# A two-layer hybrid decoder step: row-wise products that end tile by tile, a layer norm per row tile, earlier activations and regrouped transposes

## The reference

```python
def run_layer(l, x, buf_a, buf_b, h0, mem_k, mem_v):
    mix, nb_a, nb_b, h_last = token_mixing(x, ...)      # convolution, recurrence, cross-attention, w_mix_out
    x = layer_norm(ALPHA * x + mix, ln1_g[l], ln1_b[l])
    if l % 2 == 0:
        f = swiglu(x, w_ff_gate[j], w_ff_up[j], w_ff_down[j])      # d_ff = 2816
    else:
        f = moe_swiglu(x, w_router[j], ...)                        # 8 experts, top 2
    x = layer_norm(ALPHA * x + f, ln2_g[l], ln2_b[l])
```

## Time and profile before

| | us |
|---|---|
| median of 3 runs (2096.21 to 2097.61) | 2096.25 |
| profiled execution, its own time | 2094.53 |
| its span in the trace | 2092.8 |
| TensorE busy | 1944.9 (93%) |
| VectorE busy | 1488.1 (71%) |
| ScalarE busy | 1055.6 (50%) |
| GpSimd busy | 106.3 (5%) |

### The profile page before, as it was taken

The page is one execution under the profiler, slowest core; times in us unless marked ns, Lnnn a source line. Parts: engine busy times, 40 slices in busy tenths (PEclk is TensorE's granted clock), DMA queues, the critical chain, the costliest instruction groups (busy, mean ns, idle before and its releaser), DMA issues. The chain is left out here.

```text
span 2092.8 us, 27971 instructions
## 1 busy us (share of the span) xinstructions
PE 1944.9 (93%) x10429; PEld 1647.8 (79%) x10430; DVE 1488.1 (71%) x2049; ACT 1055.6 (50%) x1150; POOL 106.3 (5%) x157
## 2 busy tenths in 40 slices
PE   7999889899997999988969999999999999999990
PEld 7889789699986978978956677878787878776670
DVE  6977685565525988656567567888888888876664
ACT  4443644333322445373325445776777677665541
POOL 2000000000001020000000001010101010100000
PEclk9999999999999999999979999999999999999995
DMA  7543434254432553433337567898989898986413
GB/s 289 187 169 126 141 122 147 88 173 148 151 123 81 202 192 133 171 111 132 131 127 258 196 220 278 338 369 342 366 337 371 336 369 337 373 335 233 184 51 118
DMA packets 118597, 447.43 MB, mean 214 GB/s; under 512 B 10368, under 2 KB 10368, under 8 KB 117872
## 3 DMA queue, kind: packets, MB, share of 16 engines
q1 hardware_dynamic: 112128, 423.66, 55.7%
q0 software_dynamic: 6384, 22.64, 2.9%
HBM read 437.52 MB, written 11.36 MB: 214 GB/s over the span
## 5 line engine op out<-in xcount | busy, mean ns | idle before, releaser
L594 DVE TENSOR_TENSOR wpl<-e_ring,wph 128x2048 fp32r<-128x2048 f32 x269 | 605.8, 2286 | 87.0 <-ACT wph L588 85.4
L588 ACT CAST wph<-e_ring 128x2048 fp32r<-128x2048 f32 x269 | 502.1, 1904 | 119.8 <-PE psum L1867 66.9
L550 DVE TENSOR_TENSOR wl<-ring,wh 128x1024 fp32r<-128x1024 f32 x234 | 285.7, 1223 | 260.1 <-ACT wh L544 258.7
L1641 PE MATMUL psum<-xTh,wh 128*128 128x320 f32 x1184 | 379.2, 320 | 36.8 <-DVE xTl L1174 13.2
L1643 PE MATMUL psum<-xTh,wl 128*128 128x320 f32 x1184 | 371.3, 314 | 0.0
L1642 PE MATMUL psum<-xTl,wh 128*128 128x320 f32 x1184 | 371.2, 313 | 0.0
L544 ACT CAST wh<-ring 128x1024 fp32r<-128x1024 f32 x234 | 244.1, 1045 | 163.0 <-PE psum L1658 91.8
L1865 PE MATMUL psum<-wph,xe 128*128 128x512 f32 (+1 forms) x768 | 295.4, 385 | 3.7 <-issue 3.4
L1866 PE MATMUL psum<-wph,xe 128*128 128x512 f32 (+1 forms) x768 | 290.8, 379 | 0.0
L1867 PE MATMUL psum<-wpl,xe 128*128 128x512 f32 (+1 forms) x768 | 290.8, 379 | 0.0
L1641 PEld LDWEIGHTS psum<-xTh,wh 128*128 128x128 f32 x1184 | 227.6, 192 | 44.0 <-issue 18.4
(11 more groups left out here) (305 smaller groups left out, 2639.7 us busy)
## 6 DMA issues: line engine op xcount, KB each, us to landing
e_ring<-experts SPq DMA_DIRECT2D x264, 1024.0 KB, 6.1
ring<-stream SPq DMA_DIRECT2D x274, 512.0 KB, 3.3
lnp<-rows POOLq DMA_DIRECT2D x4, 1024.0 KB, 5.7
arena<-out_rows SPq DMA_DIRECT2D x6, 512.0 KB, 8.0
x<-x POOLq DMA_DIRECT2D x3, 512.0 KB, 13.4
arena<-x0T POOLq DMA_DIRECT2D x1, 1280.0 KB, 8.7
o_a<-arena POOLq DMA_DIRECT2D x2, 540.0 KB, 6.0
o_k<-arena POOLq DMA_DIRECT2D x2, 512.0 KB, 3.5
```

Of the source, the lines that this page charges most:

```text
L550: dve.tensor_tensor(wl[:, q % SPLITS, :], ring[:, u % SLOTS, :], wh[:, q % SPLITS, :].bitcast(F32), ALU.subtract).then_inc(lo_done, 1)
L588: act.copy(wph[:, SLOT_OF[m % NPOS], :], ring_place(m).rearrange("p u c -> p (u c)")).then_inc(hi_e, 1)
L594: dve.tensor_tensor(wpl[:, s, :], ring_place(m).rearrange("p u c -> p (u c)"), wph[:, s, :].bitcast(F32), ALU.subtract).then_inc(lo_e, 1)
L1641: pe.matmul(out, h[:, k], hi[:, k], start=(k == 0), stop=False)
```

## The change

Six edits, all in the order of work:

- `rows_of` and `Plan.rows`: the last `LAST` = 3 units are no longer used one after the other for all tiles. Unit by unit up to the fourth last; then for each row tile the three last units together. Tiles end three units' work apart instead of one's.
- `residual` does residual, statistics (`spread`) and scale (`scaled`) for one tile before the next; `normalise` is gone. At the last norm the statistics are all made first.
- the splits ahead of the norm are bounded by `last_rows`, the step at which the third last unit is used up, where the step of a tile's end stood.
- `layer_norm_std` runs a 1 x 1 square root ahead of its first wait for a variance, and with it the table load.
- the start: `x0T` is loaded by SP in two halves behind the first unit; one unit is split, four k of xTh/xTl made, the next unit split, the other four k made, the third unit split. x is loaded by GpSimd after keys and values are evacuated.
- `rows_turned` does all transposes of 128 rows of a group and then those of 32; `clear_down` multiplies zero tiles of 128 partitions.

```diff
@@ Plan.rows
-        for k in range(n_units - 1):
+        for k in range(n_units - LAST):
             self.step((), (l, name, k), split=True)
         for t in TURN:
-            last = t == TURN[-1]
-            self.step([(l, name, 2 * t), (l, name, 2 * t + 1)], (l, name, n_units - 1) if last else None, split=last)
+            if t == TURN[-1]:
+                for k in range(n_units - LAST, n_units - 1):
+                    self.step((), (l, name, k), split=True)
+            self.step([(l, name, 2 * t), (l, name, 2 * t + 1)],
+                      (l, name, n_units - 1) if t == TURN[-1] else None, split=t == TURN[-1])
@@ layer_norm_std
             act.wait_ge(eps_ready, 1)
+            act.activation(turn_top[0:1], ones[0:1, 0:1], ACT.Sqrt)
@@ sync
                 sp.dma_start(ring[:, u % SLOTS, :], stream[u]).then_inc(slot_full[u % SLOTS], 16)
+                if u == 0:
+                    for k in range(0, KT, 4):
+                        sp.dma_start(cb[:, k:k + 4], x0T[:, k:k + 4]).then_inc(xt_in[k // 4], 16)
@@ gpsimd
-            pool.dma_start(cb, x0T).then_inc(xt_in, 16)
...
                 for n in range(2):
                     emptied(pool, l, "v", n)
+                if l == 0:
+                    for t, r0 in enumerate(TOK):
+                        pool.dma_start(x[:, t, :], x0[r0:r0 + P]).then_inc(x_in, 16)
@@ scalar (vector alike, with make_lo and xTl)
-            for _ in range(SPLITS):
-                make_hi(act, queue.pop(0))
-            act.wait_ge(xt_in, 16)
+            make_hi(act, queue.pop(0))
             for k in range(KT):
+                act.wait_ge(xt_in[k // 4], 16)
                 act.copy(xTh[:, k], cb[:, k]).then_inc(xth_ready, 1)
+                if k == 3:
+                    make_hi(act, queue.pop(0))
+            make_hi(act, queue.pop(0))
...
-                split_for(tile_of(l, "mix", 0).done)
+                split_for(last_rows(l, "mix", KT))
                 layer_norm_std(act, 2 * l)
...
-                    split_for(tile_of(l, "down", 0).done)
+                    split_for(last_rows(l, "down", FT))
                     layer_norm_std(act, 2 * l + 1)
@@ vector
+            def spread(n, v, t):
+                for c in range(2):
+                    dve.bn_stats(stats[:, t, c], v[:, t, 512 * c:512 * c + 512]).then_inc(bn_done, 1)
+                dve.wait_ge(bn_done, 6 * n + 2 * TURN.index(t) + 2)
+                dve.bn_aggr(mv[:, t, 0:2], stats[:, t]).then_inc(var_ready, 1)
+            def scaled(n, v, t):
+                dve.wait_ge(std_ready, 3 * n + TURN.index(t) + 1)
+                link(dve.reciprocal(mv[:, t, 2:3], mv[:, t, 2:3]))
+                dve.tensor_scalar(v[:, t, :], v[:, t, :], mv[:, t, 0:1], mv[:, t, 2:3],
+                                  ALU.subtract, ALU.mult).then_inc(xn_ready, 1)
@@ residual, per tile t
+                    for c in range(2):
+                        emptied(dve, l, name, 2 * t + c)
+                    spread(n, x, t)
+                    scaled(n, x, t)
@@ tensor, rows_of
+                for t in TURN:
+                    for k in range(nk - LAST, nk):
+                        if t == TURN[0]:
+                            made(k)
+                        ins = unit(k, t)
+                        if t == TURN[-1] and k < nk - 1:
+                            step(ins)
+                    step(ins)
@@ rows_turned
                     pe.transpose(psum[:, b, c:c + P], rows_a[:, P * k:P * k + P], ident[:])
+                for k in range(k0, k0 + nk):
+                    c = CAP * (k - k0)
                     ins = pe.transpose(psum[:, b, c + P:c + CAP], rows_b[0:CAP_B, P * k:P * k + P],
@@ clear_down
-                        pe.matmul(psum[:, BANK_D + c, :], zero[0:32, 0:P], zero[0:32], start=True, stop=False,
+                        pe.matmul(psum[:, BANK_D + c, :], zero[:, 0:P], zero[:], start=True, stop=False,
```

More of the change, by code:

```diff
@@ L73 @@
 MEAN_AFTER = 2
+LAST = 3
 SCORES = [0, 1, 2, 3, 8, 4, 5, 6, 7, 9]
@@ L1168, in split_at @@
                 split_for(tile_of(*key).done)
-            for _ in range(SPLITS):
-                make_lo(dve, queue.pop(0))
+            make_lo(dve, queue.pop(0))
             for k in range(KT):
@@ L1619, in _ @@
             dve.wait_ge(out_first, 6)
-            normalise(2 * DEPTH - 1, x)
+            for t in TURN:
+                spread(2 * DEPTH - 1, x, t)
+            for t in TURN:
+                scaled(2 * DEPTH - 1, x, t)
             gain_bias(2 * DEPTH - 1, x)
```

84 lines of the change are left out of this document (36 added, 48 removed).

## The result

The changed kernel takes **2059.78 us** (median of four runs, 2059.09 to 2062.63) where the kernel before took 2096.23 in the same comparison (2092.15 to 2097.61): a ratio of 0.984 on record, 95% interval 0.9825 to 0.9855 (the two medians alone give 0.983). The profiled execution took 2060.36 (span 2058.6), 34.2 us less than the profiled one of before, where 28.0 were forecast.

A forecast was written before the change was run, and what follows sets the result against it. TensorE, busy 93% of the span, was taken as the bound, so only its idle or slow stretches could pay. Terms for norms, start and experts summed to 28.0 us off the 2096.25 median: 2068.2 us, range 2060 to 2079.

The forecast's parts named there:

- Sign: Whole kernel: the change makes it faster, chance 0.96; same 0.01, slower 0.03.
- Tile chain: Layer norms: 4.5 us per tile on VectorE and ScalarE; last scaled tile 5.3 after E, TensorE's last row-wise product's end.
- First norm: First layer norm: `turned_lo` starts at E + 7.6 instead of E + 12.1, -4.5 us.
- Third: Third layer norm: gain and bias start near E + 6.9 instead of E + 13.5, -6.6 us.
- The fear that the third unit's split comes late: Norms: split has a 0.3 us lead, so counted as nothing; up to 1 us per norm if that fails.
- Second norm: Norm after dense feed-forward: 6.4 us earlier, 3.6 lost as layer 1's first product waits for its moved split; -2.8 us.
- Fourth norm: Last norm, statistics to gain: table load and most of the first root's wait leave the chain, -1.2 us.
- Start: Program start: TensorE begins near 8 us, first product ends 3 to 4 earlier; -2.7 us, bounds 0.5 and 4.
- Experts, transposes: Experts: grouping by shape saves 1.3 us per turn, 1.0 in six small turns that wait 0.3; -8.6 us.
- Clearing: Experts' clearing products: the change of rows costs 0.2 us in each of eight turns; -1.6 us.
- Rival 5: Whole kernel: small turns don't wait, start and norms reach their upper bounds; 2062 us, chance 0.09.

The follow-up runs named there:

- E2: Not a run but a time mark: the end of TensorE's last row-wise product ahead of the second norm; 657.60 before, 650.91 after.
- a_za: Changed kernel, with the first unit of layer 1 split ahead of the eight activation copies at the second norm, not behind them; 2055.82 us.
- a_notable: Changed kernel without the 1 x 1 root that loads the root's table ahead of the first tile; 2067.45 us.
- a_start2: Changed kernel, with the second split at the start behind all eight activation copies instead of between the fourth and the fifth; 2058.47 us.
- both halves: Two kernels on the kernel before, grouping only a turn's last two groups of transposes or only its first; 2086.36 and 2086.83 us, one execution each.
- e_group: Kernel before, with only the experts' transposes regrouped by shape; ratio to before 0.9938.
- e_zero: Kernel before, with only the clearing products changed, to 128 partitions instead of 32; ratio to before 0.9991.
- e_norm: Kernel before, with only the norm edits: three last units tile by tile, norm per tile, split bound, early table load; ratio to before 0.9928.
- e_start: Kernel before, with only the start changed: x0T in halves, one split ahead of xTh instead of three, x loaded later; ratio to before 1.0.
- after_again: The changed kernel run once more, unchanged, beside other experiments; 2062.47 us.

## Why the prediction came out as it did

*Sign: right. Mechanism: right at the first three norms and in the experts, wrong in one step of the start and in the cause of the fourth norm, and one gain was in no step.* TensorE's idle time at the norms and its slow instructions in the experts were the price, and the edits took them away where the rows said.

*Tile chain.* "4.5 us, a little more than the 4.1 between tiles": 4.20 measured, back to back. The third scale ends at E + 4.07, not E + 5.3, and TensorE idles 1.58 us ahead of the last eight transposes, where 2 to 3 were said. First norm: `turned_lo` at E + 6.3 where E + 7.6 was worked out, so 5.8 and not 4.5, of which 5.4 are left at E2. Third: gain and bias at E + 6.3, forecast E + 6.9, before E + 13.5: 7.2 and not 6.6. About 1.0 us more there is behind the router's result: 0.8 in the chain of small products (1080.70 to 1087.99 before, 1063.22 to 1069.73 after), whose first ones now ran at the fast clock, which is a matter of the execution. The fear that the third unit's split comes late was for nothing: TensorE has no wait from it.

*Second norm.* -2.8 forecast, -3.0 measured (E2 to 794.58 against 657.60 to 804.25), by two errors that cancel, so the number is luck. The norm came 1.4 us earlier than worked out, and the displaced split cost more than 3.6: after the 8.88 us of waiting the first 12 matmuls came at the slow pace, which I had not counted. a_za shows the whole price, 4.35.

*Fourth norm.* -1.2 forecast, -1.30 measured, but not by the early root of the prediction: a_notable does without it and has the same 7.07 us. What takes the load off the chain is that each tile's aggregate now follows its own two statistics, so that the first root, and with it the load, starts while the statistics of the other tiles are still to do. The number was right for a reason that the prediction did not give.

*Start.* This step failed: "pauses for the second unit and the last four k, and ends its first product 3 to 4 us earlier". The pause was 3.35, and the matmuls behind it stayed at the slow pace up to 19.6, so the product ended little more than 1 us earlier and by the first norm nothing was left; the fourth low split, which I took for the limit (22.8 forecast, ended at 23.4), was not even waited for. a_start2 shows it by taking out the pause: 3.33 us at 71.39, 1.7 at the first norm. The lower bound of 0.5 had the cause in it ("the second unit as late as the third was"); I should have taken it, since half a megabyte stands behind 1.25 more in the same queue.

*Experts, transposes.* 1.3 per turn and a wait of 0.3 in small turns: measured 1.30 as the sum of both halves, 1.28 in the large turn of e_group, and a wait of 0.34. 0.92 per small turn against 1.0. *Clearing*: 0.20 per small turn, as forecast. Between 128-row and 32-row shapes a change costs 0.10 to 0.13 us: 0.52 for four changes fewer, 0.78 for six, 0.20 for two. The Trainium skill's two pages that the prediction sets against each other are decided by this. "TensorEngine Tiling (Array Packing)", "Key Properties", says that changing the tiling mode drains the engine, and the cost agrees with that. The weight loads pulled ahead ("TensorE: Matmul & The Clock Gate", "Step-by-step: what each phase is for") don't hide it here.

*What no step had.* About 4.5 us at the boundary behind the first large turn: 2.05 of stall and 2.4 of slow clock in e_group (stall 1.7 less in the changed kernel). The prediction read these rows for a loss that might come, and took them as fixed otherwise. e_group shows that they hang on the order of the transposes, e_zero, e_norm and e_start (stalls of 3.61, 3.46 and 4.40) that they hang on nothing else that was changed. About 1 us more of the experts' gain is phase: in the kernel before, the clock is at the lower level near 1121 and near 1900 us. In e_zero, whose transposes alternate too, it is not at the first place, and the first large turn takes 152.67 and not 153.08 us up to the transposes of its end; in e_start it is not at the second, and from the transposes at the end of the last small turn (1867.81) to the statistics it takes 199.95 and not 200.60. By the table, the experts are 4.2 us over the forecast, the third norm 1.6, the first 0.9, the second stretch 0.7, the fourth norm 0.1 and the start 1.4 under it: 6.1 of the 6.2 us between 28.0 and 34.2. Given how far stretches move on their own, only those of the experts and the first norm are sure. Rival 5 (2062) came closest, for another reason than it gave.

## What to carry to other kernels

Where an engine goes through tiles, let the end of the work come tile by tile only as far apart as the chain behind a tile is long; then look at what was queued behind the old end, because that is where the gain is lost: here the second norm gave 3.0 of 7.3 us and the start next to nothing, since a weight split stood on the wrong side of the activations' copies. Group TensorE's operations by the number of rows. Test an edit without each of its parts: the early root carries 1.3 us at three norms and nothing at the fourth. And when the forecast counts an idle stretch, it should count the slow products behind it as well.

## What the runs showed of the hardware

- **Part of an idle time is paid afterwards.** In the kernel before, the 12 matmuls behind the stall of 3.44 ran at the lower level, 1.2 GHz; its stretch in the view by windows, columns as above:

```profile
1268.41:1273.69 5.28, 5.28 (x12) 4.13 (x13) 0.06 (x2) 0.24 (x2) 1.94 (x2) 0.50 0.44 170
```

  The 12 are 0.43 us apart, the next 0.23. Behind stalls of 1.25 to 1.74 the first product is followed at 0.23 at once. In a_start2, where TensorE works on without a pause from 7.16, the pace is fast from 11.09; in the changed kernel, with the pause, from 19.6. after_again shows the pause at work: the granted clock is 1.00 from 10.5 to 13.8, 0.50 from 13.9 to 17.2 and 1.00 again from 17.3, and TensorE stands idle from 10.6 to 14.25, so the first fast stretch is lost to it. A shorter wait goes either way: behind the same wait of 2.59 us near 143 us the clock is 0.50 (143.6 to 146.9) in after_again and 1.00 in the first execution of the same program.
- **The slow stretches move between executions** of one program: 203.89 against 206.55 us for the same 1140 matmuls, at a granted clock of 0.97 and 0.95. The kernel before ranged from 2088.33 to 2097.27 in 19 runs of one comparison. A difference of 2 or 3 us in one stretch of one trace is no evidence; the same 0.20 us in five turns is.
- **Code that is first reached goes with a load of instructions.** The first small turn's first product comes 4.1 to 4.9 us after such a load begins, and the stall is what is left of that when TensorE has run dry: 1.25 to 1.74 or 3.44 to 4.40 us, by the order of the sixteen transposes ahead of it. In the kernel before, queue q8 has one more load, at 1269.3, and then none up to the end, and at no later turn is there such a stall. The cause of the two levels is open.
